# Two transformer blocks, 256 tokens, one core: four of the six gate units of w_in move into the attention

## What is computed

```python
h = modulate(rmsnorm(x, norm1_g), shift1, scale1)       # shifts, scales, gates: silu(c) @ w_ada + b_ada, 12 parts of 512
proj = h @ w_in                                         # 1024 x (4128 + 3 * 1024)
c_q, c_kv, k_pe, qkv_sb, qkv_moba, g = split(proj)      # g: 3 * 1024 columns, the gates
g = sigmoid(g)
o_mla = softmax_attention(w_uq, w_ukv of c_q, c_kv)     # 8 heads, causal
o_sb = stick_breaking_attention(qkv_sb)                 # 8 heads
o_moba = softmax_attention(qkv_moba)                    # 8 heads, causal at this length
merged = g[0] * (o_mla @ w_o_mla) + g[1] * (o_sb @ w_o_sb) + g[2] * (o_moba @ w_o_moba)
x = x + gate1 * (merged @ w_out)
x = x + gate2 * (relu(modulate(rmsnorm(x), shift2, scale2) @ w_ff1) ** 2 @ w_ff2)
```

## Time and profile before

| | us |
|---|---|
| median of 3 runs | 1919.32 (1913.68 to 1922.93) |
| profiled execution, its time | 1914.08 |
| its span, first to last instruction | 1912.4 |
| PE busy / DVE busy / ACT busy | 1740.9 / 1175.2 / 841.0 |

### The profile page before, as it was taken

The page is one execution under the profiler, slowest core; times in us unless marked ns, Lnnn a source line. Parts: engine busy times, 40 slices in busy tenths (PEclk is TensorE's granted clock), DMA queues, the critical chain, the costliest instruction groups (busy, mean ns, idle before and its releaser), DMA issues.

```text
span 1912.4 us, 25470 instructions
## 1 busy us (share of the span) xinstructions
PE 1740.9 (91%) x9675; PEld 1447.8 (76%) x9675; DVE 1175.2 (61%) x2164; ACT 841.0 (44%) x1475; POOL 124.1 (6%) x272
## 2 busy tenths in 40 slices
PE   6999978979999999879799989797999898979998
PEld 6798755579987887554699868665998686649996
DVE  4877444566657876454545575563778655637885
ACT  2245344245434453361355343362555444625553
POOL 1000011000000000120000010040000100400000
PEclk8999999989999999999899989898999898889999
DMA  9787710438765977303356646503665465026552
GB/s 320 258 280 256 240 55 23 135 115 288 261 190 186 323 257 258 131 1 120 101 191 202 192 122 210 153 2 112 186 182 184 144 195 161 8 88 186 180 186 88
DMA packets 185610, 323.75 MB, mean 169 GB/s; under 512 B 13492, under 2 KB 101136, under 8 KB 185488
## 3 DMA queue, kind: packets, MB, share of 16 engines
q1 hardware_dynamic: 183184, 321.59, 52.0%
q10 hardware_dynamic: 2304, 0.52, 0.1%
HBM read 321.02 MB, written 1.05 MB: 168 GB/s over the span
## 4 chain that ended last, share of the span: by engine, by line
PE 75%; DVE 13%; ACT 5%; issue 2%; POOL 2%; DMA 2%; SPq 0%; DVEq 0%; ACTq 0%
PE bank L621 72%; PE bank L630 3%; DVE ring_r L1466 3%; DVE sm L1609 1%; POOL sm L571 1%; DMA ring<-in_w_in 1%; DMA x<-in_x 1%; ACT high L1114 1%; DVE ada L1547 1%; DVE wide L1459 1%; DVE mx L1615 0%; DVE oT L1518 0%; POOL stat L564 0%; DVE wide L1869 0%; ACT pT L1211 0%
## 5 line engine op out<-in xcount | busy, mean ns | idle before, releaser
L1466 DVE TENSOR_TENSOR ring_r<-ring,high 128x1024 fp32r<-128x1024 f32 (+3 forms) x428 | 507.5, 1199 | 343.2 <-ACT high L1114 334.0
L1114 ACT ACTIVATE high<-ring 128x1024 fp32r<-128x1024 f32 (+3 forms) x428 | 442.5, 1039 | 557.1 <-PE bank L621 449.0
L621 PE MATMUL bank<-featT_r,high 128*128 128x256 f32 x1216 | 349.6, 288 | 16.3 <-DVE oT_r L1498 14.5
L621 PE MATMUL bank<-oT_r,high 128*128 128x256 f32 x1216 | 348.2, 286 | 0.0
L621 PE MATMUL bank<-featT_r,ring_r 128*128 128x256 f32 x1216 | 347.9, 286 | 0.0
L621 PE MATMUL bank<-ring_r,featT_r 128*128 128x464 f32 (+3 forms) x736 | 282.6, 384 | 0.0
L621 PE MATMUL bank<-high,featT_r 128*128 128x512 f32 (+3 forms) x672 | 260.1, 387 | 11.8 <-DVE oT_r L1498 7.4
L621 PE MATMUL bank<-high,gates_r 128*128 128x512 f32 x864 | 268.0, 390 | 2.0 <-DVE ring_r L1466 1.2
L621 PE MATMUL bank<-high,oT_r 128*128 128x512 f32 (+3 forms) x672 | 255.4, 380 | 0.0
L621 PEld LDWEIGHTS bank<-featT_r,high 128*128 128x128 f32 x1216 | 237.8, 196 | 18.4 <-issue 16.0
L621 PEld LDWEIGHTS bank<-oT_r,high 128*128 128x128 f32 x1216 | 238.0, 196 | 0.0
(11 more groups left out here) (231 smaller groups left out, 1854.0 us busy)
## 6 DMA issues: line engine op xcount, KB each, us to landing
ring<-in_w_ff SPq DMA_DIRECT2D x128, 512.0 KB, 4.4
ring<-in_w_ada SPq DMA_DIRECT2D x96, 512.0 KB, 6.1
ring<-in_w_up SPq DMA_DIRECT2D x176, 256.0 KB, 3.2
ring<-in_w_in SPq DMA_DIRECT2D x64, 464.0 KB, 5.3
ring<-in_w_in SPq DMA_DIRECT2D x48, 512.0 KB, 6.7
ring<-in_w_in SPq DMA_DIRECT2D x48, 474.0 KB, 4.0
ring<-in_w_down SPq DMA_DIRECT2D x44, 512.0 KB, 3.5
ring<-in_w_out SPq DMA_DIRECT2D x24, 512.0 KB, 4.7
```

What stands on the lines that cost most here:

```text
L621: ins = pe.matmul(o, a, b, start=start, stop=stop, skip_group_check=True)
L1114: act.activation(it["high"], it["raw"], ACT.Copy).then_inc(high_ready, 1)
L1466: dve.tensor_tensor(it["low"], it["raw"], it["high"].bitcast(F32), ALU.subtract).then_inc(low_ready, 1)
```

## The change

Of the gates, units 0 and 1 (w_in units 9 and 10) stay where they were. The other four, eight token tiles, go into attention as whole tiles into the banks `outputs`: one after the transposes of the first softmax part, one each after the scores of its steps 1 and 4; one after the transposes of stick breaking and one each in its steps 3 and 4; one each in steps 2 and 4 of the last softmax part. DVE copies a tile to `gates` without the sigmoid (`gates_out`), and after the last part ACT applies the sigmoid in place to 4 x 1024 columns (`gates_ready`). The weight pieces of these units come in the stream from behind w_uq on; ACT makes their high parts, and DVE the low parts, two at a time at the beginning of steps of the parts.

Since the features `featT_r` and `featL` must now outlive attention, the latent features and the queries and keys of the first part go into free columns of `gates` (`lat`), and the outputs of heads into `proj` and `kvm` (`out_of`). The modulation parts 10 and 11 leave w_in for w_ff1 of the same layer: `FF_STEPS` of layer 0 goes from one unit with four pieces to five such, that of layer 1 from none to four units with two.

```diff
-        IN_STEPS = [4, 4] + [2] * 12
-        IN_OUT = {1: 4, 2: 5, 4: 6, 6: 7, 8: 8, 10: 9, 12: 10, 14: 11}
-        FF_STEPS = [4, 2, 2, 2, 2, 2, 2, 0]
-        FF_OUT = {1: 0, 3: 1, 5: 2, 7: 3}
+        IN_STEPS = [4, 4] + [2] * 8
+        IN_OUT = {1: 4, 2: 5, 4: 6, 6: 7, 8: 8, 10: 9}
+        FF_STEPS = [[4, 4, 4, 4, 4, 2, 2, 0], [2, 2, 2, 2, 0, 0, 0, 0]]
+        FF_OUT = [{1: (0, 10), 2: (0, 11), 3: (1, 0), 4: (1, 1), 5: (1, 2), 7: (1, 3)}, {2: (1, 10), 4: (1, 11)}]
...
-            for u in range(15):
+            for u in range(11):
...
+            gate_unit = split(w_in[l], (ATT + 2 * 512, ATT + 3 * 512), later=True)
             for u in range(2):
                 plain(cols_piece(w_ukv[l], 0, KVR // P, (512 * u, 512 * u + 512)))
+            for it in gate_unit:
+                used(it)
+            for u in range(3, 6):
+                split(w_in[l], (ATT + 512 * u, ATT + 512 * u + 512))
...
+        MLA_FILL, SB_FILL, MOBA_FILL = (1, 4), (3, 4), (2, 4)
...
@@ PE
+            def gate_quarters():
+
+                for _ in range(4):
+                    get, n = next_quarters()
+                    for t in range(T):
+                        b, _n = claim(outputs)
+                        for j in range(QUARTERS):
+                            w = get(j)
+                            for kk in range(2):
+                                c = 2 * j + kk
+                                three(b[:, 0:n], feature_parts(c, slice(t * P, t * P + P)), (w[0][:, kk, :], w[1][:, kk, :]),
+                                      c == 0, c == KD - 1, outputs.full if c == KD - 1 else None)
+                            if t:
+                                owed.append((piece_used, 1))
+                            yield
...
-                turns(mla_turns)
-                softmax_heads(mla_jobs)
-                turns(sb_turns)
-                stick_heads()
+                quarters = gate_quarters()
+                during = lambda *steps: lambda i: gates_tile(quarters) if i in steps else None
+                turns(mla_turns, lambda: gates_tile(quarters))
+                softmax_heads(mla_jobs, None, during(*MLA_FILL))
+                turns(sb_turns, lambda: gates_tile(quarters))
+                stick_heads(during(*SB_FILL))
                 turns(moba_turns)
-                softmax_heads(moba_jobs)
+                softmax_heads(moba_jobs, None, during(*MOBA_FILL))
@@ ACT
+                highs(4)
                 for u in range(2):
...
-                softmax_heads(mla_jobs)
+                softmax_heads(mla_jobs, lambda i: highs(2 if i in (2, 3) else 0))
                 turns_out(sb_turns)
-                stick_heads(l)
+                stick_heads(l, lambda i: highs(2 if i in (0, 1) else 0))
                 turns_out(moba_turns)
-                softmax_heads(moba_jobs)
+                softmax_heads(moba_jobs, lambda i: highs(2 if i in (0, 1) else 0))
+                act.wait_ge(outputs.read, gates_tile0[l])
+                for br in (1, 2):
+                    for t in range(T):
+                        g = gates[:, t, br * D:(br + 1) * D]
+                        act.activation(g, g, ACT.Sigmoid).then_inc(gates_ready, 1)
@@ DVE
+            def gates_out():
+
+                n = next(gate_cols)
+                b = tile(outputs)
+                read(outputs, dve.tensor_copy(n, b[:, :]))
...
+                gates_out()
+                softmax_heads(mla_jobs, lambda i: first_quarters(2 if i in (2, 3) else 0), MLA_FILL)
                 turns_out(sb_turns)
-                stick_heads()
+                gates_out()
+                stick_heads(lambda i: first_quarters(2 if i in (1, 2) else 0), SB_FILL)
                 turns_out(moba_turns)
-                softmax_heads(moba_jobs)
+                softmax_heads(moba_jobs, lambda i: first_quarters(2 if i in (0, 1) else 0), MOBA_FILL)
...
                     if br:
                         first_quarters(2)
+                        seen.more(gates_ready, T)
```

More of the change, by code:

```diff
@@ L296, in cols_piece, with used, put @@
             return piece(k1 - k0, at, parts, reader, split)
-        def put(it, spare=None):
+        uses = {"pe": 0, "dve": 0}
+        def used(it):
+            uses[it["reader"]] += 1
+            it["turn"] = uses[it["reader"]]
+        def put(it, spare=None, later=False):
             u = len(stream)
@@ L302, in put @@
             before = stream[u - RAW]["loaded"] if u >= RAW else 0
-            it.update(slot=u % RAW, loaded=before + 16 * len(it["parts"]),
-                      turn=1 + sum(1 for o in stream[:u] if o["reader"] == it["reader"]))
+            it.update(slot=u % RAW, loaded=before + 16 * len(it["parts"]))
+            if not later:
+                used(it)
             for key, of in (("raw", ring), ("low", ring_r)):
@@ L330, in ada_piece, with split @@
             put(it)
-        def split(w, *cols, rows=(0, KD), per=2, beside=0, spare=None):
+        def split(w, *cols, rows=(0, KD), per=2, beside=0, spare=None, later=False):
             pieces = [cols_piece(w, k0, k0 + per, *cols, split=True) for k0 in range(rows[0], rows[1], per)]
@@ L376, in two_blocks @@
             more = l + 1 < LAYERS1
-            ada_of_layer = ada_order(l + 1, 0, 4) if more else None
+            ada_of_layer = itertools.chain(ada_order(l, 10, 12), ada_order(l + 1, 0, 4) if more else ())
             for u in range(8):
-                split(w_ff1[l], (512 * u, 512 * u + 512), beside=FF_STEPS[u - 1] if u and more else 0)
+                split(w_ff1[l], (512 * u, 512 * u + 512), beside=FF_STEPS[l][u - 1] if u else 0)
             for u in range(8):
@@ L1158, in features_out @@
             def features_out(gain=None, shift=None, parts=False, tiles=range(T)):
-                dst = featF if parts else featT
                 for t in tiles:
@@ L1292, in _ @@
                 sums(proj[:, :, QR:QR + KVR], 16, KVR)
-                for u in range(6):
+                for u in range(2):
                     for t in range(T):
@@ L1476, in first_quarters @@
             def first_quarters(n):
-                if not begun:
+                if n and not begun:
                     begun.extend(next(cut))
```

118 lines of the change are left out of this document (73 added, 45 removed).

## The result

The changed kernel takes 1926.86 us (median; 1924.32 to 1929.55), the kernel before 1919.32 (1913.34 to 1922.93) in the same series: ratio 1.0040, 95% interval 1.0025 to 1.0055. It is slower by 7.5 us, less than half a per cent, where 4 us less was forecast. The profiled execution took 1924.32, to be set against 1914.08 before and the 1910.0 of the sum.

What follows compares the result with a forecast made beforehand. PE was taken as the bound, busy 1740.9 of 1912.4 us. Terms -1.6 - 6.6 + 5.1 - 1.0 gave -4.1: 1910.0 against the profiled 1914.08, or 1915 on the median's basis; own range 1908 to 1922, with rivals 1898 to 1931.

Steps and rivals of the forecast that it cites:

- parts 1 and 2: Dense part against returning tiles and products, -0.8 a layer (-1.6); waits covered in attention, 3.3 a layer (-6.6).
- part 4: Tables: the sigmoid's load in layer 1's dense part goes, -1.0; three new loads in the second block taken as 0.
- part 2: Attention: gate tiles cover PE's waits, upper bound 10.6 a layer, net 3.3 after losses, -6.6 for two layers.
- The bank claims of the outputs: Stick breaking: tiles share two output banks with the pairs' outputs, so a claim waits about 1.3, twice.
- the third step of stick breaking: Attention: PE's wait in this step should grow from 1.87 to near 4.
- Rival A: Attention: all 10.6 us of waits a layer vanish; 1900.6, with the clock 1895; chance 0.31.
- part 3: Modulation beside w_ff1: layer 0 pays 1.2 in each of four units, 4.8; layer 1 0.3; together +5.1.
- Rival B: w_ff1 of layer 0: ring starves, 4 to 4.5 us in each of five units, about +20, 1930; chance 0.20.
- Rival C: Second block and end of attention: table switches with drain on the path, 2.66 each, 1927; chance 0.05.
- The last layer's w_ff1: Layer 1's w_ff1: two modulation pieces a unit, which cost nothing in layer 0; 0.3 counted.
- the named signs: Attention without the tiles' 44 about 67 us each, 60 under rival A; shrinking by more than 5 a layer means wrong.
- The sign for w_ff1: Layer 0's w_ff1: 5 to 8 longer, waits near 1 us in five units; no waits at all means wrong.

Runs made afterwards that it cites:

- experiment 3: The changed kernel with the exp and ln table loaded on ACT right behind the last sigmoids of layer 1; ratio to the kernel before 1.0040.
- experiment 1: The kernel before with only modulation parts 10 and 11 moved beside w_ff1, attention untouched; ratio to the kernel before 1.0103.
- experiment 4: The kernel before, unchanged, profiled a second time; 1923.75 us in one execution.
- experiment 10: The changed kernel with modulation parts 10 and 11 beside the three last gate units in attention, DVE's pieces behind the low parts; ratio to the kernel before 1.0077.
- experiment 11: The changed kernel with parts 10 and 11 beside the four gate units in attention, DVE's pieces placed where it waits for a tile; 1907.87 us, ratio 0.9948.

## Why the prediction was wrong

On its own basis the sum said 1910.0, and the execution took 1924.3: 14.3 more. Term by term:

**Dense part and waits covered (parts 1 and 2, and the table load of part 4): right.** Forecast -13.2 over both layers (tiles, covered waits, the table load), measured -16.0. The idle time that went is 3.2 and 3.0 a layer, where I had 3.3. The eight tiles were priced too high: 44.0 a layer, where busy PE grew by 43.2 and 41.5. In layer 1 the granted clock over the stage is 0.97, against 0.95 before; I had put no gain from it in the sum. The pieces of part 2 were right too, save one. The bank claims of the outputs cost 1.32 twice, as worked out (about 1.3). The turn before the last part stayed at 1.8, and of POOL's 3.9 in both softmax parts 1.4 are left. But the third step of stick breaking did not wait near 4: it has 2.06, while the waits on POOL's mask before it went from 1.2 to 2.1 in sum. Rival A, attention as PE's own with all 10.6 covered, did not happen.

**The modulation beside w_ff1 (part 3): the step that failed.** I had 4.8 us of new waits and 2.0 of products in layer 0, 6.8 in all; it was 19.1. The failed sentence is "In four of them a modulation product of about 0.95 follows the unit before and hides half: 0.9 a unit", with "In a row of such units I count 0.3 more each". Measured were 3.5, 3.2, 2.8 and 2.6 a unit, and 0.5 in the one after, 12.7 in place of 4.8. The other 4.4 are busy PE: 105.4 us against 99.0, two of them products. I had not thought of the clock here. In the kernel before it is 1.00 over the same part of w_ff1, which is the first of these rows. In the changed kernel, the second and third, it fell twice to 1.2 GHz, behind waits of 2.41 and 2.59 us:

```profile
470.00:502.00 32.00, 32.00 (x269) 32.00 (x269) 21.73 (x25) 17.07 (x21) 0.00 (x0) 1.00 0.78 270
464.00:480.00 16.00, 13.74 (x104) 13.24 (x102) 9.29 (x13) 6.57 (x8) 0.00 (x0) 0.90 0.70 247
480.00:496.00 16.00, 15.26 (x114) 15.04 (x115) 10.08 (x13) 7.94 (x10) 0.00 (x0) 0.89 0.68 245
```

What the clock withheld in these two stretches, 0.10 and 0.11 of 16 us, makes up to 3.4 of the 4.4; no row here shows the remaining 1.0. The forecast had nothing for either.

I took the price of the waits from the one such unit before, which has the ring full ahead of it and a unit with two pieces behind it, and scaled it. In a row, the pieces of each unit are requested in the second half of a unit that was itself full, and the loop of request, landing, high and low part closes on PE, at the third and fourth quarter of the next unit. What the product between two units hides of that is not shown: no run has such a row without the products. The earlier trace rows already showed the wait of 3.00 on a late piece; I counted it unseen because a light unit followed. The same row, followed by another full unit, was the forecast.

**Rival B was the nearest.** Its place and its sign hold. Its 20 us are to be set against 17.1 (19.1 less the two products), and its 4 to 4.5 a unit against waits of 2.6 to 3.5 in four units, which stay under the 3.7 from which it was to decide. That its 1930 lies 3 above the measured median is in part luck, since 5.2 of the measured time come from the second block, which it did not have either. Its reason holds in part. It had a piece land 12.8 us after its request (6.7 + 6.1), at 311 GB/s as the rate of a full stretch; the pieces landed after 3.8 to 7.4. The transfers reach 403, and the mean over the stage is 228 in the changed kernel as against 231 before. Thinning the loads took away 4.1 of the 12.7 us of new waits; DVE's products and the timing of the slots count as much. I gave it 0.20 because "the rate can be higher in short stretches". The rate is higher, and the stage starves all the same.

**Tables (part 4): right.** The three loads in the second block were taken as 0 and cost 0.4 us (experiment 3). Rival C is not borne out: neither PE's wait (0.42 more) nor the spacing of the loads (1.52) has room for its price of a switch. That price is from the Trainium skill, ScalarE: Activation LUTs, "What ACT_TABLE_LOAD costs", which gives 1.28 us for the load and 1.38 for a drain, 2.66 in all. The trace agrees with the load and shows no room for the drain. The 12 us that I gave for this price were also off, as four switches at 2.66 make 10.6.

**The second block: not in the sum at all.** It gives +5.2 in the profile. Experiments 1, 3 and 4 show that it is not the tables (0.4 of it), and that two profiles of the kernel before agree within 0.1 over the stretch from the fox product to the output product. That stretch holds 3.0 of the 5.2; what differs in it is the granted clock, 0.89 against 0.85 in the changed kernel. Why the clock is lower there is open. I had looked for the clock only inside attention.

**The last layer's w_ff1** got 1.9 longer against 2.3 forecast, with no new waits, as two pieces a unit were said to cost nothing.

Of the named signs, attention without the tiles' 44 is 66.3 and 64.4, nearer to the 67 than to the 60 of rival A. In layer 1 that is 5.5 less than before, just over the 5 that I had named as a sign of being wrong, but 2.5 of it is the price of the tiles and not covered waits. The sign for w_ff1, no waits at all, was on the wrong side: the failure was too many. The waits of ACT for w_ff pieces near 3 us repeat, which was the sign of rival B.

## What to carry to other kernels

The price of a full unit, read from one that has light units around it, is not the price of a row of them. Write down which slot each load of the next unit needs and in which half of the present one it comes free, and follow one full turn of the loop. Beside a chain of engines, added work is free or paid in full by its place: 12.2 us of DVE work made attention about 12 a layer longer ahead of the masks (experiment 10; 7 to 10 of it waits of PE, the rest its clock) and cost nothing that shows in DVE's waits for a tile (experiment 11), so move such work to the row where its engine waits for the bottleneck. Compare waits before lengths where the granted clock differs between two profiles: leaving out DVE's products shortened w_ff1 by 1.7 us and its waits by 4.8. And profile an unchanged kernel twice before explaining a stage that the change does not touch.

## What the hardware showed that was not expected

- The transfers ran at up to 403 GB/s in slices of 3 us and fell to 3 to 24 between, with the same mean of some 230 GB/s that the quick stage had: the mean rate over a stage said nothing about starvation.
- A block whose code no edit touches ran at a granted clock of 0.89 in both profiles of the kernel before and at 0.85 to 0.87 in kernels edited elsewhere (+2.7 us on 76.8 in experiment 1). A shift in time alone did not do it, as the second profile of the kernel before reached the block 9.5 us later and kept 0.89. A difference of this size there says nothing of the edit's own work.
- In a row of stalls in one product, PE's granted clock fell to 1.2 GHz behind waits of 2.41 and 2.59 us and not behind those of 2.38 and 2.10 us in the units before, so the same edit cost some 3.4 us beyond its waits.
